# Thirty experts in 12 turns of two or three, in place of 15 turns of two

## The reference

```python
logits = (xt @ w_router + b_router)              # 256 tokens, 32 experts
top_v, top_e = lax.top_k(logits, 4)              # 4 experts for each token
gates = softmax(top_v)
# for each expert e, on the tokens that chose it:
y = clamped_swiglu(xb @ w1[e] + b1[e]) @ w2[e] + b2[e]   # w1 1024x2048, w2 1024x1024
```

## Time and profile before

| | |
|---|---|
| median of 3 runs | 2652.26 us (2649.83 to 2655.31) |
| profiled execution, its own time | 2649.32 us |
| its span | 2647.5 us |
| TensorE matmul busy | 2388.3 us (90%) |
| VectorE busy | 1448.4 us (55%) |
| ScalarE busy | 633.9 us (24%) |
| bytes moved by DMA | 711.89 MB |
| mean granted TensorE clock | 0.967 of full speed |

### The profile page before, as it was taken

One profiled execution on the slowest core, in us unless ns is written; L12 is line 12 of the kernel. 1 busy time (PEld: TensorE's weight loads), 2 busy tenths in 40 slices (PEclk: granted clock), 3 DMA queues, 4 the chain that ended last, 5 costly groups with the idle time before them and its releaser, 6 DMA issues.

```text
span 2647.5 us, 43597 instructions
## 1 busy us (share of the span) xinstructions
PE 2388.3 (90%) x18084; PEld 1596.5 (60%) x18084; DVE 1448.4 (55%) x2805; ACT 633.9 (24%) x795; POOL 111.1 (4%) x195
## 2 busy tenths in 40 slices
PE   6998988999999899888889898899998999996998
PEld 5887633444444453345445454477767987774897
DVE  2446445444343343555444444576668766776876
ACT  1111211122121121111111111133443433332432
POOL 0000010000000000000000000000000000000000
PEclk8999999999999999999999999999999999998999
DMA  8788888988999799888989888543435542322652
GB/s 345 297 309 328 325 349 328 363 351 349 390 361 368 301 376 373 346 309 324 364 311 365 324 351 319 220 167 139 155 127 207 190 143 98 110 98 88 221 185 77
DMA packets 111249, 711.89 MB, mean 269 GB/s; under 512 B 12480, under 2 KB 13136, under 8 KB 36128
## 3 DMA queue, kind: packets, MB, share of 16 engines
q1 hardware_dynamic: 85904, 616.93, 60.1%
q0 software_dynamic: 25168, 92.38, 9.8%
HBM read 705.06 MB, written 4.19 MB: 268 GB/s over the span
## 4 chain that ended last, share of the span: by engine, by line
PE 74%; DVE 19%; issue 3%; ACT 3%; DMA 1%; DVEq 0%; SPq 0%; ACTq 0%
PE bank L269 25%; PE bank L2176 6%; PE bank L2157 5%; PE bank L1894 5%; PE bank L1932 4%; PE bank L1909 3%; PE bank L1559 3%; PE bank L1416 2%; PE bank L2042 2%; DMA ring<-in_units_a 1%; PE bank L2261 1%; PE bank L1818 1%; PE bank L2031 1%; PE bank L2073 1%; DVE scratch L2938 1%
## 5 line engine op out<-in xcount | busy, mean ns | idle before, releaser
L269 PE MATMUL bank<-hid,scratch 128*32 128x512 f32 x816 | 339.3, 595 | 0.0
L269 PE MATMUL bank<-hT,scratch 128*32 128x512 f32 x784 | 336.3, 597 | 0.0
L1188 ACT CAST chi<-craw 128x1024 fp32r<-128x1024 f32 x128 | 133.3, 1043 | 581.2 <-PE bank L1894 172.4
L3158 DVE TENSOR_TENSOR clo<-craw,chi 128x1024 fp32r<-128x1024 f32 x128 | 155.6, 1221 | 41.7 <-ACT chi L1188 41.0
L269 PE MATMUL bank<-yacc,scratch 128*32 128x512 f32 x1128 | 175.1, 597 | 0.0
L269 PE MATMUL bank<-diag_gtmp,scratch 128*32 128x512 f32 x1128 | 173.2, 592 | 0.0
L269 PE MATMUL bank<-rows,scratch 128*32 128x512 f32 x1112 | 172.5, 600 | 0.0
L269 PE MATMUL bank<-cst,scratch 128*32 128x512 f32 x1112 | 170.4, 593 | 0.0
L1894 PE MATMUL bank<-cT_hi,chi 128*128 128x256 f32 x384 | 116.6, 304 | 40.2 <-DVE crot_lo L3132 17.2
L2948 DVE TENSOR_SCALAR scratch<-bank 128x512 f32<-128x512 f32 x32 | 22.1, 692 | 217.9 <-PE bank L269 217.9
L2944 DVE TENSOR_SCALAR scratch<-bank 128x512 f32<-128x512 f32 x32 | 22.1, 692 | 210.0 <-PE bank L269 210.0
(11 more groups left out here) (664 smaller groups left out, 6045.5 us busy)
## 6 DMA issues: line engine op xcount, KB each, us to landing
hid<-in_panels_e SPq DMA_DIRECT2D x96, 1024.0 KB, 9.9
hT<-in_panels_e SPq DMA_DIRECT2D x94, 1024.0 KB, 9.8
ring<-in_units_a SPq DMA_DIRECT2D x88, 1024.0 KB, 7.3
ring<-in_panels_m SPq DMA_DIRECT2D x64, 1024.0 KB, 5.1
yacc<-in_panels_e SPq DMA_DIRECT2D x48, 1024.0 KB, 6.7
diag_gtmp<-in_panels_e SPq DMA_DIRECT2D x48, 1024.0 KB, 8.8
rows<-in_panels_e SPq DMA_DIRECT2D x47, 1024.0 KB, 7.2
cst<-in_panels_e SPq DMA_DIRECT2D x47, 1024.0 KB, 8.3
```

The costliest lines, as they stand in the source:

```text
L269: m = self.pe.matmul(b[s:s + STRIP, :], lhs(k)[:, s:s + STRIP], v, start=(first and k == 0), stop=(k == KT - 1))
L1188: act.copy(chi[:, h % 2, :], context_raw(h)).then_inc(cx_hi, 1)
L3158: tt(context_lower(h), context_raw(h), chi[:, h % 2, :], ALU.subtract).then_inc(cx_lo, 1)
```

## The change

There are 12 sorted turns in place of 15. Even ones have two experts (96 and 32 slots), odd ones have three (64, 32 and 32 slots): 6 x 2 + 6 x 3 = 30 experts. By their number of tokens, the six largest get 96 slots, the next six 64, and the other eighteen 32. The list of overflowing experts and its loop stay, with `MORE` 18; one further turn now loads its expert once and not twice.

The eight half places are now single places in rotation: load m goes to place (m - 4) mod 8 once the 12 first places are used up, and SP waits for the half panel that used it eight loads before. A step (a half panel of a turn) of a three-expert turn takes three places. SP's loop over turns is written out. There are twelve points in a turn in place of six, also between the two halves of a panel, and the same 148 pieces are dealt to them by weights of 7 for a point of a three-expert turn and 5 for one of a two-expert turn. From `context_points`, the odd turns then get 14, 15, 14, 15, 14 and 13 pieces (12, 12, 12, 15, 14, 13 units), the even ones 11 and then 10 each (7, 9, 8, 4, 10, 10 units). What else changes follows from these (`places` and `weights` go over two or three experts, table `tab_p`, one more comparison in `order_started`, `pg` a tile of its own, the semaphores of landing counted by place, `nat_in` replaced by `first_in`).

```diff
 STRIP = 32
 MANY = 96
 STATIC = 2
-TURNS = (32 - STATIC) // 2
+SHARES = ((MANY, SLOTS - MANY), (64, 32, 32)) * 6
+FIRST_SHARES = (SLOTS // 2, SLOTS // 2)
+TURNS = len(SHARES)
...
-MORE = 16
+MORE = 18
...
-POINTS = 6
+POINTS = 12
+HELD = 12
...
-def place_of(n):
-
-    return n if n < 3 else (n - 1) % 2
+def first_of(turn):
+
+    return sum(len(shares) for shares in SHARES[:turn])
+
+
+def load_of(turn, j, h):
+
+    before = 0 if turn < 0 else 12 * (len(FIRST_SHARES) + first_of(turn))
+    return before + (2 * j + h) * (len(FIRST_SHARES) if turn < 0 else len(SHARES[turn]))
+
+
+STATIC_LOADS = load_of(TURNS - 1, 0, 0) + 12 * len(SHARES[-1])
+STEPS = [(panel, h) for panel, shares in ((6 * (turn + 1) + j, shares) for turn, shares in enumerate((FIRST_SHARES,) + SHARES, -1)
+                                          for j in range(6)) for h in range(2) for _ in shares]
+
+
+def place_of(m):
+
+    return m if m < HELD else (m - 4) % 8
+
+
+def use_of(m):
+
+    return 1 if m < HELD else (m - HELD) // 8 + 2
+
+
+def user_before(m):
+
+    return STEPS[m - 12 if m < 20 else m - 8]
...
     at = [[] for _ in range(number + 2)]
+    share = [7 if len(SHARES[n // POINTS]) == 3 else 5 for n in range(number - 1)]
+    ends = [sum(share[:n + 1]) for n in range(number - 1)]
     for n in range(len(pieces) - 2):
-        at[n * number // (len(pieces) - 2)].append(n)
+        at[next(k for k, end in enumerate(ends) if n * ends[-1] < end * (len(pieces) - 2))].append(n)
...
+    def begin(self, turn, shares):
+
+        self.at_turn, self.shares, self.j = turn, shares, 0
+        self.owner = [p for p, n in enumerate(shares) for _ in range(n // STRIP)]
...
+        m = load_of(self.at_turn, self.j, h)
+        panels = []
+        for n in range(m, m + len(self.shares)):
+            s = place_of(n)
+            self.pe.wait_ge(self.landed[s], (16 if s < 8 else 32) * use_of(n))
+            panels.append(self.places[s])
+        return panels
+
+    def rows(self, b, lhs, first, h):
+
+
+        panels = self.halves(h)
+        for k in range(4 * h, 4 * h + 4):
+            for n, s in enumerate(range(0, SLOTS, STRIP)):
+                v = panels[self.owner[n]][:, k % 4, :]
                 m = self.pe.matmul(b[s:s + STRIP, :], lhs(k)[:, s:s + STRIP], v, start=(first and k == 0), stop=(k == KT - 1))
...
-    at = np.where(e < 2 * TURNS, np.where(e % 2 == 0, e // 2, 2 * TURNS - 1 - e // 2), e)
+    at, smalls = [], iter(range(TURNS, EXPERTS))
+    for turn, shares in enumerate(SHARES):
+        at += [turn // 2 + (TURNS // 2) * (turn % 2)] + [next(smalls) for _ in shares[1:]]
+    at = np.array(at + list(smalls))
...
         def _(sp):
-            def panels_of_two(both, loads):
-
-                for h, used in enumerate((E["half0"], E["done"])):
-                    sp.wait_ge(used, loads.at(-2 if loads.n in (3, 4) else -1))
-                    for p in range(2):
-                        half_panel(both[p], place_of(loads.n), p, h)
-                loads.n += 1
+            released = {0: 0, 1: 0}
+
+            def next_half(src, m, h):
+
+                panel, half = user_before(m)
+                if released[half] < panel + 1:
+                    sp.wait_ge((E["half0"], E["done"])[half], panel + 1)
+                    released[half] = panel + 1
+                half_panel(src, m, h)
...
-            with turns(sp, TURNS, {loads: 6}) as i:
-                both = [sp.value_load(order_e[0:1, bass.ds(i * 2 + p, 1)], min_val=0, max_val=EXPERTS - 1) for p in range(2)]
+            for turn, shares in enumerate(SHARES):
+                who = [sp.value_load(order_e[0:1, first_of(turn) + p:first_of(turn) + p + 1], min_val=0, max_val=EXPERTS - 1)
+                       for p in range(len(shares))]
                 for j in range(6):
-                    panels_of_two([at(pe_, e * 6 + j) for e in both], loads)
+                    for h in range(2):
+                        for p, e in enumerate(who):
+                            next_half(at(pe_, e * 6 + j), load_of(turn, j, h) + p, h)
...
-            def expert_pair(many=MANY, start=False, point=None):
+            def expert_turn(shares, turn=None, start=False, point=None):
                 beside = (lambda n: None) if point is None else (lambda n: context(point + n))
+                EG.begin(turn, shares)
                 EA.read()
-                first_product(0, many)
+                first_product(0, lambda: beside(0))
...
-                beside(0)
-                first_product(1, many)
+                beside(1)
+                first_product(1, lambda: beside(2))
...
                     combine(1)
-                beside(1)
-                first_product(2, many)
+                beside(3)
+                first_product(2, lambda: beside(4))
                 turn_act(0)
-                beside(2)
-                first_product(3, many)
-                beside(3)
+                beside(5)
+                first_product(3, lambda: beside(6))
+                beside(7)
...
                 gather()
-                beside(4)
+                beside(8)
                 EM.read()
-                second_product(half, many, range(4, KT))
+                second_product(b, 1)
                 turn_gathered(0)
                 turn_gathered(1)
-                beside(5)
-                second_product(EG.open(), many)
+                beside(9)
+                b = EG.open()
+                second_product(b, 0)
+                beside(10)
+                second_product(b, 1)
+                beside(11)
...
-                estep(ts(extra, rank, float(TURNS), float(2 * MANY - SLOTS), ALU.is_lt, ALU.mult))
+                for n, first in enumerate((TURNS // 2, TURNS)):
+                    m = ts(rs[:, 10 + n:11 + n], rank, float(first), float(STRIP), ALU.is_lt, ALU.mult)
+                estep(m)
+                estep(tt(extra, rs[:, 10:11], rs[:, 11:12], ALU.add))
```

More of the change, by code:

```diff
@@ L250, in halves @@
     def halves(self, h):
[L252 to L268, removed]
+        if self.at_turn is None:
+            r = 2 * self.j + h
+            landings = self.panels.turn * 48 + 16 * (LAST_USE[r % 4] + r // 4 + 1)
+            self.pe.wait_ge(self.landed[r % 4], landings)
+            return [self.places[r % 4]] * len(self.shares)
@@ L621, in program @@
         feat_ready = sem("feat_ready")
-        nat_in = [sem(f"nat_in{n}") for n in range(4)]
+        first_loads = [16 * len(range(n, len(first_units()), 4)) for n in range(4)]
         nat_hi = sem("nat_hi")
@@ L638, in expert_sems @@
                 )
-        E = expert_sems("e_", len(wide))
+        E = expert_sems("e_")
+        ring_landed = [sem(f"ring_landed{h}") for h in range(2)]
+        panel_landed = E["landed"] + [ring_landed[0]] * 2 + [ring_landed[1]] * 2
         cbank = bank[2:4]
@@ L746, in program @@
         E0 = 5064
-        pg = carve(5056, 2, 2, 2)
         GD = carve(E0, 2, SLOTS)
@@ L922, in _ @@
             more = sp.value_load(more_i[0:1, 0:1], min_val=0, max_val=MORE)
+            further = Count(6 * (TURNS + 1))
             with sp.If(more > 0):
-                with turns(sp, more, {loads: 6}) as i:
+                sp.wait_ge(E["done"], further.n)
+                with turns(sp, more, {further: 6}) as i:
                     e = sp.value_load(list_e[0:1, bass.ds(i, 1)], min_val=0, max_val=EXPERTS - 1)
                     for j in range(6):
-                        panels_of_two([at(pe_, e * 6 + j)] * 2, loads)
-                sp.wait_ge(E["done"], loads.at())
+                        for h, used in enumerate((E["half0"], E["done"])):
+                            sp.wait_ge(used, further.at(-1))
+                            s = (2 * j + h) % 4
+                            sp.dma_start(panel_places[s], at(pe_, e * 6 + j)[:, h * UNIT:(h + 1) * UNIT]
+                                         .rearrange("p (k n) -> p k n", k=4)).then_inc(panel_landed[s], 16)
+                        further.n += 1
+                sp.wait_ge(E["done"], further.at())
                 sp.sem_inc(further_done, 1)
@@ L1832, in first_product, with second_product @@
                 pe.matmul(b[:, :], chosen[:, :], b1t[:, col:col + 512], start=True, stop=False)
-                EG.rows(b, lambda k: xg[:, k, :], many, False)
-            def second_product(b, many, depths=range(KT)):
-                EG.rows(b, lambda k: aT[:, k, :], many, True, depths)
+                for h in range(2):
+                    EG.rows(b, lambda k: xg[:, k, :], False, h)
+                    if h == 0:
+                        middle()
+            def second_product(b, h):
+                EG.rows(b, lambda k: aT[:, k, :], True, h)
             def turn_act(c, sent=1):
@@ L1992, in _ @@
             counts = {EG.c: 6, EG.panels: 6, EA.c: 4, EH.c: 2, EM.c: 6, from_experts.c: 3}
-            expert_pair(SLOTS // 2, start=True)
+            expert_turn(FIRST_SHARES, turn=-1, start=True)
             for i in range(TURNS):
```

(26 more changed lines are left out.)

110 lines of the change are left out of this document (57 added, 53 removed).

## The result

The changed kernel takes 2461.6 us (median of four runs, 2460.5 to 2463.8) against 2651.9 us; the ratio is 0.928, interval 0.927 to 0.930. That is 190 us less. Forecast were 2505 us and -147, with 2460 to 2585 as the range.

What follows compares the result with a forecast made beforehand. TensorE was taken to set the turn, DMA some 13% behind. Six pairs of 188 us (182 plus 6 added) made 1128 against 1275, -147: 2502 profiled, 2505 as median; 2480 to 2540, with two rivals 2460 to 2585.

Steps and rivals of the forecast that it cites:

- What bounds the kernel before: Sorted turns: TensorE sets the turn, busy 91% of 1275 us; DMA share 0.87, the two bounds some 13% apart.
- Three turns' own work, 154 us: TensorE in the sorted turns: three turns fewer remove 3 x 51.2 = 154 us; context work stays at 388.
- Idle time, 4.5 us a turn: TensorE: with twelve points, pieces' lower parts are made one point earlier, so idle falls from 7.9 to 4.5 us a turn.
- my upper bound: TensorE's idle time: the most twelve points could save, all of 7.9 us a turn but the 1.4 before `gather`.
- New waits, 7 us a three-expert turn: TensorE in three-expert turns: DMA falls behind, so some 7 us of new waits for loads, from step 5 or 6 on.
- The pair of 182 us: One three-expert turn at 101.5 us and one two-expert turn at 80.5, before 6 us a pair was added.
- 36 that I added: Six pairs of sorted turns: 6 us a pair for lower clock and late context loads; bounds none and 15 a pair.
- The late units: Context loads to ScalarE: its waits, 71.7 us for one kind, grow with DMA full; part of the 6 us a pair.
- Waits vanish, DMA alone counts: Rival for the sorted turns: each pair costs only its bytes, 181 us; -189, 2463 us; chance 0.09.
- No evening out: Rival: three-expert turns pay their whole 109 us, two-expert turns 84, a pair 198; -87, 2565 us; chance 0.21.
- The rate isn't there: Rival: DMA can't pass its mean of 344 GB/s, so no change, 2649 us; at 358 GB/s 2593; chance 0.03.
- overflow turn: Rival: an expert passes 32 tokens; each further turn costs about 59 us, two make 2623; chance 0.03.

Runs made afterwards that it cites:

- the kernel with fewer bytes: The kernel before, its expert loads in the fifteen sorted turns bringing three of four depths; 2654.5 us, ratio 1.000.
- the deals: The changed kernel with other weights for context pieces in three- and two-expert turns: 6 : 6 took 2469.8 us, 4 : 8 2554.6, 9 : 3 2463.2.
- six-point run: The changed kernel with its context pieces at only the six old places of a turn, weights 7 and 5 kept; 2574.7 us, ratio 0.970.
- fewer-bytes run: The changed kernel with three of four depths in every expert load of the twelve sorted turns; 2423.3 us, ratio 0.914.
- eleven-turn run: The changed kernel with eleven turns, three of two experts and eight of three, same experts and bytes; 2451.0 us, ratio 0.923.
- blocked order: The changed kernel with first six turns of two experts, then six of three, in place of alternating; 2475.0 us, ratio 0.933.

## Why the prediction held, point by point

**The number.** 2461.6 us lies 2 us inside the stated range, and below the 2480 to 2540 that the forecast itself stood for. The range reached so far down only because it took in a rival with a chance of 0.09. The direction, the size of the removed work and the form of the new waits were foreseen; that the range held at its edge is luck.

**What bounds the kernel before.** Right: the kernel with fewer bytes is not faster.

**Three turns' own work, 154 us.** TensorE's busy time fell by 153, but two errors cancel in that. In the fifteen-turn kernel with twelve points, at a granted clock of 1.00, the same subtraction of the context work gives (1135 - 388) / 15 = 50 us for a turn's own work. The 51.2 held 22 / 15 = 1.5 us of the slower clock of the earlier trace rows, which I had counted as work. So three turns are 150 us and the points gave 22 more; 19 us came back, as the changed kernel is busy 1004 us at 0.98 and not 1135 - 150 = 985. Differences between runs give less, (1134 - 990) / 3 = 48 from fifteen to twelve turns and 990 - 946 = 44 from twelve to eleven, all with fewer bytes; along them the granted clock falls from 1.00 to 0.99 and 0.98, so they are not own work alone. So the 48 that the expectations of the deals used is probably too low.

**Idle time, 4.5 us a turn.** In the changed kernel it is (84.4 - 29.7) / 12 = 4.6 beside the waits for panels. The number is right and its reason is not: with one piece at each point fifteen turns show 1.8 a turn, near my upper bound, all but the 1.4 before `gather`. The rest goes with points that carry two pieces, 14 in the twelve turns; over the deals it grows with their number.

**New waits, 7 us a three-expert turn.** 29.7 / 6 = 5.0. They stand where I had them, in three-expert turns alone, and begin 44 to 57 us after the last `y_hi` of the turn before, in the first such turn after 24. The pair of 182 us that I had at this point of the working, counted like the 85.0 of before over the stretch, is 1088.4 / 6 = 181.4. For single turns I had 104 and 83; they took 100 and 85.

**Where it failed.** The stretch in the sum is 996 us of TensorE's work, 54 of idle time, 42 of waits for panels and 36 that I added, 6 a pair, for lower clock and late context units: 1128. Measured are 1004 + 55 + 30 = 1088. The step that failed is the 36; waits too large by 12 and work too small by 8 nearly cancel. The other 4 of the 43 us between forecast and result are the profiled run, which now lies 2.2 us above the median where I had it 2.9 below, less 1 us outside the stretch.

The clock's part of it is real, and smaller. A product behind a wait of 2.64 us runs at nearly half speed, one behind 2.22 us does not; the two 10 us slices have clocks of 0.83 and 1.00:

```profile
523.63 1.02 PE L310 MATMUL bank<-yacc,scratch 128*32 128x512 f32 x2 [2.64 <-DMA diag_gtmp<-in_panels_e]
749.72 0.62 PE L310 MATMUL bank<-yacc,scratch 128*32 128x512 f32 x2 [2.22 <-DMA diag_gtmp<-in_panels_e]
```

```profile
523.00:533.00 10.00, 8.68 (x45) 4.06 (x46) 0.00 (x0) 1.65 (x3) 0.54 (x1) 0.83 1.01 419
748.00:758.00 10.00, 6.92 (x49) 3.84 (x50) 2.87 (x7) 0.92 (x3) 0.33 (x1) 1.00 1.02 422
```

Five of the 18 waits, of 1.9 to 3.3 us, are followed by the lower level, 1.2 GHz; by the 0.83 each costs about 1.7 us. In all TensorE is busy 14 us longer than with fewer bytes, 2.4 us a pair. But my 51.2 us a turn already held a clock of 0.97, and the stage is at 0.98, so there was nothing to add for the clock. The rule of the Trainium skill (TensorE: Matmul & The Clock Gate, HAM oscillation) that stretches of products can start cold after a wait for DMA is borne out at those five waits, and not at the other thirteen; it doesn't come every time here. The six-point run, with 172 us of idle time, has 0.95.

The late units are nothing. ScalarE's waits for them did grow, from 164 us to 349:

```profile
ACT chi L1248 <- DMA craw<-in_panels_m: 210.6, 38, 8.7
...
ACT chi L1248 <- DMA craw<-in_units_b: 138.1, 27, 8.1
```

But in the fewer-bytes run, where DMA has 13% to spare and these waits are 221 us, TensorE's idle time beside the panels stays at 54 us. A unit that was late for ScalarE was not late for TensorE; by the lists, half a panel of products lies between a cast and its use.

**The rivals.** *Waits vanish, DMA alone counts* gave 2463, and the time is that. Its bound is the right one: a pair is its bytes, 181 us, and one turn less of TensorE work gives 11 us of 41. That it fits to 2 us is in part chance, as its rate of 410 GB/s lies between the 405 that the eleven-turn run held and the 420 of single slices. Its picture of TensorE is wrong: the waits didn't vanish, they lie where the bytes have to be waited for anyway. I had added what the two sides cost instead of taking the larger. *No evening out* is what the blocked order makes of it: 108.4 us for a three-expert turn, against the 109 worked out from bytes, but 13 us in all and not 60, since a two-expert turn took 80 and not the 84 of that rival. *The rate isn't there* fell: 405 GB/s stood for 1076 us in the eleven-turn run. The Trainium skill's 358 GB/s per core (DMA: Bandwidth & Descriptors, Specifications) is under what this core had by itself. No overflow turn ran, and the mean clock of the stage didn't fall.

**Where the gain is.** From the kernel before, 116 us come by the twelve points alone (with the new places and the written-out loop) and 79 by the turns alone, or with the points in place 77. That the two nearly add up to 190 is chance: with six points the turns' gain goes to doubled points, and with twelve 35 us of it go to the bytes.

## What to carry to other kernels

When side work is woven into an engine's list, give each piece a place of its own and prepare its operands one place earlier; here this, with the places that came along with it, gave 116 us, more than taking away a fifth of the turns, 77. Before work is taken from the engine that sets the time, divide the bytes of the stage by the rate of a long stretch with full engines (410 GB/s before, 405 held afterwards, though single slices reach 420): that is near the floor, and when both sides come near it, the larger of the two counts, not their waits added up. An idle time that moves from one cause to another under equal times is the mark of a bound that is neither of them.

## What the runs showed of the hardware

In the eleven-turn run the DMA engines held 405 GB/s over 1076 us at share 1.00, with loads of 1 MB from one queue and of 0.5 MB from another. In the changed kernel, at share 0.99 in place of 0.87, the expert loads' median times to landing rose from 6.7 to 10.0 us to 10.5 to 13.1. The same TensorE work took 22 us longer (1157 for 1135) with 118 us of idle time at six points of a turn than with 27 us at twelve. Waits for panels of 1.9 to 3.3 us were followed by half the clock five times (2.64, 2.15, 3.27, 1.93 and 2.03 us), while others up to 2.50 us were not.
